# Ten input projection tiles of a two-block transformer kernel, unsplit and between the steps of its delta-rule stage

## The reference, cut to what matters

```python
proj = h @ w_in
qkv_a, z_a, b_a, a_a, qkv_b = split(proj)       # 1536, 512, 4, 4, 1536 columns
qkv_a = silu(causal_dwconv(qkv_a, conv_qkv_w))  # 4 heads of 128: gated delta rule
qa = l2norm(qa) * 128 ** -0.5;  ka = l2norm(ka)
g = -exp(a_log) * softplus(a_a + dt_bias);  beta = sigmoid(b_a)
o_a = rmsnorm(gated_delta_rule(qa, ka, va, g, beta)) * silu(z)
o_b = dilated_attention(qb, kb, vb)             # 8 heads of 64, from qkv_b
x = x + concat([o_a, o_b]) @ w_out
```

## Time and profile before

| | |
|---|---|
| three runs | 2054.92, 2056.27, 2057.14 us; median 2056.27 |
| the profiled execution | 2054.92 us, span 2053.1 us |
| busy over the span | TensorE 96%, its weight loads 77%, VectorE 62%, ScalarE 39% |
| instructions | 35683 |
| DMA | 164.68 MB, mean 80 GB/s |

### The profile page before, as it was taken

The page is one execution under the profiler, slowest core; times in us unless marked ns, Lnnn a source line. Parts: engine busy times, 40 slices in busy tenths (PEclk is TensorE's granted clock), DMA queues, the critical chain, the costliest instruction groups (busy, mean ns, idle before and its releaser), DMA issues.

```text
span 2053.1 us, 35683 instructions
## 1 busy us (share of the span) xinstructions
PE 1970.2 (96%) x15123; PEld 1587.1 (77%) x15123; DVE 1276.1 (62%) x2192; ACT 810.2 (39%) x1268; POOL 0.2 (0%) x4
## 2 busy tenths in 40 slices
PE   7998888899999999999999999999999999999998
PEld 6876555568888886788888888888887685888886
DVE  7622677557557565677777777777777734344444
ACT  5364333543334344534433443433434424332323
POOL 0000000000000000000000000000000000000000
PEclk9999899999999999999999999999999999999998
DMA  6331322233333322221211112121122441223221
GB/s 180 93 89 35 104 84 89 88 104 105 100 93 92 103 83 74 83 63 53 62 54 53 53 52 63 53 63 53 53 62 73 155 129 56 72 83 93 82 82 52
DMA packets 286160, 164.68 MB, mean 80 GB/s; under 512 B 6348, under 2 KB 283570, under 8 KB 286002
## 3 DMA queue, kind: packets, MB, share of 16 engines
q1 hardware_dynamic: 285492, 162.22, 26.8%
q10 hardware_dynamic: 510, 0.18, 0.0%
HBM read 160.29 MB, written 2.10 MB: 79 GB/s over the span
## 4 chain that ended last, share of the span: by engine, by line
PE 90%; DVE 5%; ACT 3%; issue 1%; DMA 0%; ACTq 0%; SPq 0%; DVEq 0%
PE bank L485 21%; PE bank L487 20%; PE bank L486 20%; PE bank L502 2%; PE bank L503 2%; PE bank L504 2%; PE bank L927 2%; PE bank L1092 1%; PE bank L975 1%; PE bank L958 1%; PE bank L468 1%; PE bank L549 1%; PE bank L547 1%; PE bank L548 1%; PE bank L935 1%
## 5 line engine op out<-in xcount | busy, mean ns | idle before, releaser
L485 PE MATMUL bank<-hh,wh 128*128 128x512 f32 x1384 | 562.1, 406 | 0.0
L1162 ACT ACTIVATE wh<-stage 128x1024 fp32r<-128x1024 f32 (+1 forms) x246 | 257.2, 1048 | 747.7 <-PE bank L487 489.2
L1686 DVE TENSOR_TENSOR wl<-stage,wh 128x1024 fp32r<-128x1024 f32 (+1 forms) x246 | 298.4, 1215 | 402.9 <-ACT wh L1162 402.9
L487 PE MATMUL bank<-hh,wl 128*128 128x512 f32 x1384 | 541.1, 391 | 0.0
L486 PE MATMUL bank<-hl,wh 128*128 128x512 f32 x1384 | 540.5, 391 | 0.0
L487 PEld LDWEIGHTS bank<-hh,wl 128*128 128x128 f32 x1384 | 260.1, 188 | 56.5
L485 PEld LDWEIGHTS bank<-hh,wh 128*128 128x128 f32 x1384 | 260.4, 188 | 55.5 <-issue 3.9
L486 PEld LDWEIGHTS bank<-hl,wh 128*128 128x128 f32 x1384 | 260.9, 188 | 48.7 <-issue 1.0
L485 PE MATMUL bank<-gh,wh 128*128 128x512 f32 x324 | 126.7, 391 | 0.0
L487 PE MATMUL bank<-gh,wl 128*128 128x512 f32 x324 | 126.2, 389 | 0.0
L486 PE MATMUL bank<-gl,wh 128*128 128x512 f32 x324 | 126.1, 389 | 0.0
(11 more groups left out here) (392 smaller groups left out, 2828.7 us busy)
## 6 DMA issues: line engine op xcount, KB each, us to landing
stage<-in_hg_w_in SPq DMA_DIRECT2D x80, 512.0 KB, 3.6
stage<-in_ada_w SPq DMA_DIRECT2D x48, 512.0 KB, 4.1
stage<-in_w_up SPq DMA_DIRECT2D x44, 512.0 KB, 3.7
stage<-in_ft_w_in SPq DMA_DIRECT2D x32, 512.0 KB, 3.9
stage<-in_w_in SPq DMA_DIRECT2D x28, 512.0 KB, 3.8
stage<-in_w_down SPq DMA_DIRECT2D x16, 512.0 KB, 3.9
stage<-in_hg_w_out SPq DMA_DIRECT2D x16, 512.0 KB, 4.2
stage<-in_ft_w_out SPq DMA_DIRECT2D x16, 512.0 KB, 4.0
```

Of the source, the lines that this page charges most:

```text
L485: pe.matmul(bank[t % NLIN][:], wh[:, s, k, :], xh[:, k, :], start=a, stop=False)
L487: mm = pe.matmul(bank[t % NLIN][:], wl[:, s, k, :], xh[:, k, :], start=False, stop=b)
L1162: do(A.activation(wh[:, l % NSPLIT, 0:nk, :], stage[:, u["slot"], 0:nk, :], ACT.Copy), "hi_ready")
L1686: do(X.tensor_tensor(wl[:, l % NSPLIT, 0:nk, :], stage[:, u["slot"], 0:nk, :], wh[:, l % NSPLIT, 0:nk, :].bitcast(F32), ALU.subtract), f"s ...
```

## The change

Tiles 18 to 27 leave the projection loop; `T_IN` is 18. The loop keeps qkv_a, z, and queries and keys of head pair 0 (`FIRST_PAIR`). The ten others (`MIDS`: queries and keys of pairs 1 to 3, values of all pairs) become "mid" units, computed unsplit, eight blocks each (one per slice k), between the steps of the delta-rule stage, by a table `FILL` (blocks placed early and late in step n). Values are computed with the tokens on partitions at once, so their transposes go. All mids accumulate in bank 2, ScalarE copies each finished tile (`mid_copy`). The raw units no longer sit in the odd steps but where `MOD_STEP` puts them, and the list of units, with it the order of loads and the slots, is interleaved anew. VectorE makes the whole activations (`whole_h`, eight sums) in chunk 0. The column sums are now two groups of four, after tiles 9 and 12, and use four banks and parts of `bqkv`; squares are taken after tiles 6 and 10; the gate products come after tiles 5, 7 and 14. Some buffers of the stage move so that `hh` and `hw` stay intact.

In the diff the wait on `mid_ev` by `(3, 6, 9, 10)[hp]` is `weigh`'s; the two pairs of `fill_first` and `fill_last` stand in step 0 (and so in step 7) and, behind T, in steps 1 to 6.

```diff
+T_IN = 18
+FIRST_PAIR = (0, 4)
+MIDS = (1, 5, 8, 2, 6, 9, 3, 7, 10, 11)
+FILL = {0: (1, 1), 1: (1, 2), 2: (1, 2), 3: (1, 2), 4: (1, 2), 5: (1, 1), 6: (1, 2), 7: (1, 2), 8: (1, 1),
+        11: (1, 3), 12: (1, 3), 13: (1, 3), 14: (1, 3), 15: (1, 3), 16: (1, 3),
+        19: (1, 3), 20: (1, 3), 21: (1, 3), 22: (1, 3), 23: (1, 3), 24: (1, 3),
+        27: (1, 3), 28: (1, 3)}
+MID_END = {2: 0, 5: 1, 8: 2, 12: 3, 14: 4, 16: 5, 20: 6, 22: 7, 24: 8, 28: 9}
+MOD_STEP = {1: 0, 3: 1, 5: 2, 7: 3, 9: 4, 10: 5, 17: 6, 18: 7,
+            24: 8, 25: 9, 26: 10, 27: 11, 28: 12, 29: 13, 30: 14, 31: 15}
...
+    mids = [dict(w="w_in", rows=(0, 8), col=O_B + m * P, lin=False, mid=i) for i, m in enumerate(MIDS)]
+    done = 0
+    for n in range(32):
+        step = []
+        if n in MOD_STEP:
+            step.extend(raws[2 * MOD_STEP[n]:2 * MOD_STEP[n] + 2])
+        if n in FILL:
+            if done % 8 == 0:
+                step.insert(0 if n % 8 in (0, 7) else len(step), mids[done // 8])
+            done += sum(FILL[n])
+        units.extend(step)
...
-                if t in range(16, 24, 2):
-                    col_sum(t - 16)
-                    col_sum(t - 15)
+                if t in (9, 12):
+                    for i in range(4):
+                        col_sum(i + (4 if t == 12 else 0))
...
-            for a in range(TT):
...
-                for j in range(4):
-                    mm = pe.transpose(bank[1 + a % 2][:, j * P:(j + 1) * P], bqkv[:, 8 + j, a * P:(a + 1) * P], ident[:])
-                mm.then_inc(S("vb_T"), 1)
+            def fill(n):
+                for _ in range(n):
+                    i, k = fed[0] // KT, fed[0] % KT
+                    fed[0] += 1
+                    u = mid_units[i]
+                    slot = u["slot"]
+                    if k == 0:
+                        pe.wait_ge(S(f"stage_in{slot}"), 16 * (u["load"] + 1))
+                        if i:
+                            pe.wait_ge(S("mid_ev"), i)
+                        if i >= 3:
+                            pe.wait_ge(S("ob_lo"), i // 3)
+                    if i == 0:
+                        pe.wait_ge(S("h_whole"), k + 1)
+                    if MIDS[i] < 8:
+                        mm = pe.matmul(bank[2][:], stage[:, slot, k, :], whole(k), start=(k == 0), stop=(k == KT - 1))
+                    else:
+                        for a in range(TT):
+                            mm = pe.matmul(bank[2][:, a * P:(a + 1) * P], hw[:, k, a * P:(a + 1) * P], stage[:, slot, k, :],
+                                           start=(k == 0 and a == 0), stop=(k == KT - 1 and a == TT - 1))
+                    if k == KT - 1:
+                        mm.then_inc(S(f"stage_free{slot}"), 1)
...
+                pe.wait_ge(S("mid_ev"), (3, 6, 9, 10)[hp])
...
                 attention_tail(n)
+                fill_first(n)
                 pe.wait_ge(S("eex"), c + 1)
...
                 scores(n + 1)
                 modulation(n)
+                fill_last(n)
...
                     modulation(n)
+                    fill_first(n)
                     attention_tail(n)
...
                     scores(n + 1)
+                    fill_last(n)
...
+            def mid_copy(n):
+                if n in MID_END:
+                    i = MID_END[n]
+                    u = mid_units[i]
+                    act.wait_ge(S(f"stage_free{u['slot']}"), u["load"] + 1)
+                    do(A.activation(bqkv[:, MIDS[i], :], bank[2][:], ACT.Copy), "mid_ev")
...
+            def whole_h(k):
+                do(X.tensor_tensor(whole(k), hl[:, k, :].bitcast(F32), hh[:, k, :].bitcast(F32), ALU.add), "h_whole")
```

More of the change, by code:

```diff
@@ L122, in make_units @@
     late = raws[32:]
-    for t in range(28):
-        add("w_in", (0, 8), t * P if t < 16 else O_B + (t - 16) * P, "h")
-    units.extend(raws[:32])
+    for t in range(T_IN):
+        add("w_in", (0, 8), t * P if t < 16 else O_B + FIRST_PAIR[t - 16] * P, "h")
+    mids = [dict(w="w_in", rows=(0, 8), col=O_B + m * P, lin=False, mid=i) for i, m in enumerate(MIDS)]
[9 more added lines that the diff above has]
+        units.extend(step)
     for n in range(KT):
@@ L335, in build @@
         T_OUT, T_UP, T_HG, T_HO, T_FT = FIRST["w_out"], FIRST["w_up"], FIRST["hg_w_in"], FIRST["hg_w_out"], FIRST["ft_w_in"]
-        MOD_STEP = {1 + 2 * j: j for j in range(16)}
         LATE_STEP = {0: 16, 1: 17, 2: 18, 3: 19, 5: 20, 6: 21, 7: 22, 8: 23}
-        late_units = [u for u in units if not u["lin"] and u["raw"] >= 32]
-        raw_last = {u["raw"] // 2: u for u in units if not u["lin"]}
+        raw_units = [u for u in units if "raw" in u]
+        late_units = raw_units[32:]
+        mid_units = [u for u in units if "mid" in u]
+        raw_last = {u["raw"] // 2: u for u in units if "raw" in u}
         WHOLE = {t: i for i, t in enumerate((T_UP, T_HG))}
@@ L590, in col_sum @@
                 pe.wait_ge(S("l2_sq"), i + 1)
-                if i >= 2:
-                    pe.wait_ge(S("l2_ln"), i - 1)
-                pe.matmul(bank[4 + i % 2][:], ones[:], sq[:, i % 2, :], start=True, stop=True
+                if i >= 4:
+                    pe.wait_ge(S("l2_ln"), i - 3)
+                pe.matmul(bank[4 + i % 4][:], ones[:], l2buf(i), start=True, stop=True
                           ).then_inc(S("l2_sum"), 1)
@@ L714, in modulation @@
                 if step in MOD_STEP:
-                    for _ in range(2):
-                        unit(units[pos[0]])
-                        pos[0] += 1
+                    for i in range(2):
+                        unit(raw_units[2 * MOD_STEP[step] + i])
             def attention_tail(n):
@@ L823, in _ @@
             weigh(3)
+            assert fed[0] == KT * len(MIDS)
+            pos[0] += 32 + len(MIDS)
             assert units[pos[0]]["lin"]
@@ L1298, in _ @@
             do(A.activation(silp[:, :, 1], V[:, ROWS["c_ctx"][0]:ROWS["c_ctx"][0] + 8], ACT.Silu), "silc_ready")
-            def square_pair(i, last):
-                if i < last:
-                    for n in (i, i + 1):
-                        col_square(n, qkv[:, n, :])
-            for t in range(28):
+            for t in range(T_IN):
                 finish_tile(t)
@@ L1345, in _ @@
                     do(A.activation(egc, bank[3][:, 80:96], ACT.Exp), "gate_act")
-            for a in range(TT):
-                act.wait_ge(S("vb_T"), a + 1)
-                do(A.activation(bqkv[:, 8:12, a * P:(a + 1) * P], bank[1 + a % 2][:].rearrange("p (j c) -> p j c", c=P), ACT.Copy), "vb_ev")
             def weights(n):
@@ L1781, in _ @@
             do(X.memset(raw[:, :, 0:3], 0.0), "set_dve")
-            for t in range(12):
+            for t in range(T_IN):
                 weights_behind(t)
@@ L1875, in _ @@
                 front(8 * c)
+                if c == 0:
+                    whole_h(2)
+                    whole_h(3)
                 dve.wait_ge(S("eex"), c + 1)
@@ L1889, in _ @@
                 do(X.copy_predicated(G["xt"][:], view(gmask[:, 0, :], [[0, 4], [1, P]]), G["lt"][:]), "x1")
+                if c == 0:
+                    for k in range(4, KT):
+                        whole_h(k)
+                    dve.wait_ge(S("h_whole"), KT)
                 dve.wait_ge(S("vk"), c + 1)
```

150 lines of the change are left out of this document (79 added, 71 removed).

## The result

The changed kernel takes **2068.56 us** (median of four runs, 2067.31 to 2069.41) against 2056.7 for the kernel before (2054.92 to 2057.15): ratio 1.0052, 95% interval 1.0035 to 1.0068. It is slower by some 12 us. The forecast was 2051.0 with a range of 2041 to 2063, so sign and range were both missed. On a second chip the same two kernels gave 1.0028 (1.0016 to 1.0040): slower again, by less. The profiled execution took 2069.41 us, span 2067.6.

The account below looks back on a forecast made before the run. TensorE was taken to bound the projection, with neither TensorE nor VectorE full in the delta-rule stage. Projection -57.4 plus stage +53.2 gave -4.2 us, 2050.7 against the profiled 2054.9; median put at 2051, range 2041 to 2063.

Parts of the forecast that it names:

- the clock behind the four waits for loads: Delta-rule stage, steps 3, 9, 25, 29: the sum counted the waits' idle time only, no slower clock behind them.
- front: Input projection up to the first scores: 28 tiles become 18 and value transposes go, -57.4 us, bounds -60 to -53.
- length of the waits: TensorE's idle time for late modulation loads and step 3's next tile weights: 11.6 us in all.
- the rest of the stage: Delta-rule stage less its load waits: 230.9 us of the 242.5 forecast, blocks and VectorE's new sums included.
- behind the stage: Everything after the delta-rule stage keeps its slots and its order: 0 us.
- rival D: ScalarE's chain between tiles 9 and 14 is longer by up to six table loads, 7.7 us: 2058.4 us; chance 0.04.
- The places of the waits: Modulation loads held by a projection tile's slot are waited for in steps 3, 9, 25 and 29.
- landing of 3.9 us: Held-back modulation loads land 3.9 us after the last product of the tile holding their slot, signal included.
- the half loss of clock counted at steps 9, 17 and 25: Steps behind the heads of chunks 1 to 3: blocks shorten the idle hole, so half the old clock loss stays.
- rival B: Clock stays at 2.4 GHz where blocks are dense and falls at no load wait: 6.0 us less, 2044.7; chance 0.27.
- Rival C: Clock falls at the four slot waits and again at each head, dense work at 1.2 GHz: +10.8, 2061.5; chance 0.20.
- Rival E: Stage hides nothing, blocks fully added to the old 189.3 us: +23.7, 2078.6 us; chance 0.02.

Follow-up runs that it names:

- e5: Changed kernel with the ten tiles' loads placed anew and the modulation of steps 3 and 5 moved to steps 2 and 4: 2041.98 us, ratio 0.9911.
- e3: Changed kernel with useless TensorE products put ahead of the awaited loads in steps 3, 9, 25 and 29: 2056.95 us, ratio 0.9984.
- e7: Kernel before the change, with three useless 512-column products in each chunk head ahead of the turned first inverse: ratio 0.9990.
- e8: e5 with the last of the ten tiles at place 33 of the load queue, not 34: ratio 0.9959.
- e6: Changed kernel with blocks moved into TensorE's holes, mainly chunk heads, loads and three modulation steps placed to suit: 2032.55 us, ratio 0.9865.
- e11: e6 with the two last blocks of step 1 moved to the end of chunk 0's head: 2030.82 us, ratio 0.9874.
- e4: Changed kernel with loads reordered, modulation steps moved and seven of eight blocks of each moved tile left out: 2019.39 us, ratio 0.9794.

## Why the prediction was wrong, step by step

The step that failed is the clock behind the four waits for loads: the forecast put it at nothing, and it measured +17.3 us. The other terms came out at -0.1 (front), +2.0 (length of the waits), -0.8 (the rest of the stage) and +0.2 (behind the stage) beside the forecast.

**The front was right.** Forecast -57.4, measured -57.5. ScalarE's chain was in time. The wait at tile 14 was 1.08 us where 2.3 were forecast:

```profile
120.82 0.40 PE L698 MATMUL bank<-gs,cst 128*128 128x16 f32 x2 [1.08 <-DVE gs L1870]
```

So rival D is out. By the 1.38 us of drain at each table load that the Trainium skill states (ScalarE: Activation LUTs, "What ACT_TABLE_LOAD costs") the chain would, as an estimate, have ended 8.3 us later. The trace disagrees: the wait is 1.08 us.

**The places of the waits were right, their length nearly.** The four steps were 3, 9, 25 and 29, with the next tile's weights late in step 3, as worked out. The sum was 13.6 us for 11.6, +2.0. The mis-sized term is the landing of 3.9 us, and it shows in two of the five: 4.20 us at step 9 for 3.0, and 1.91 for the next tile's weights in step 3 for 0.85. The others measured 2.69, 2.65 and 2.15 for 3.0, 2.5 and 2.2. The forecast took a load as it lands alone or in a pair, but a held-back slot releases three or four loads at once, and then they share the engines: the median landing of the modulation weights is 5.3 us in the changed kernel and 4.1 in e5, where no slot holds a burst back.

**The stage without its waits was right, by two errors that cancel.** The sum has 242.5 - 11.6 = 230.9 us without the waits; e5 has 230.1, though with two modulation steps moved. The blocks were dearer: groups of three ran at 2.77 us from the first to the next T, so 0.92 each, with single ones at 0.95 to 0.97, where 0.854 was taken from the inside of a dense tile. That is some 4 us over 80.

```profile
234.44 2.84 PE L720 MATMUL bank<-hw,stage 128*128 128x512 f32 x6
237.21 0.46 PE L829 MATMUL bank<-g_xx,g_lt 128*32 128x32 f32 x32
```

Against it, the half loss of clock counted at steps 9, 17 and 25 is absent where no wait comes: e5's steps 9, 17 and 25 take 5.4, 5.4 and 6.0 us. That is rival B's point, and it holds for a kernel that wasn't the one measured.

**The clock behind the waits was the miss.** The profiled stage is 18.5 us above the sum: +2.0 for the waits, -0.8 for the rest, +17.3 for slower products (18.4 by the busy sums; some 1 us of those lay where TensorE would have idled). By chunks against e5, with the waits taken off: 66.1 - 59.0 - 4.6 = 2.5; 62.7 - 55.8 - 4.2 = 2.7; 58.7 - 57.1 = 1.6; 73.5 - 58.2 - 4.8 = 10.5. Rival C had this mechanism and the sign, with 2.5, 1.4, 2.1 and 4.8. It got a chance of 0.20 and a price too low in chunk 3, where it assumed a fall of a few microseconds, and the fall outlasted steps 30 and 31. The argument in the record was in the wrong place. It let the clock fall behind the heads by precedent, and the earlier trace rows, and for the slot waits, as long and as idle, it counted the idle time only. Its one case against a fall was an idle 2.16 us in dense work; at 2.15 us idle the clock did fall here. Had the falls behind the waits been counted, C would have been the main line: 2061.5, still 8 us short of the profiled 2069.4. The forecast also named the heads as the place of all falls before; three others stood there, with no wait over 0.93 us ahead of them.

The rule of the Trainium skill beside it, that the clock follows how busy TensorE has lately been (TensorE: Matmul & The Clock Gate, "What's actually happening"), agrees in direction with e3 and e7, where useless work brought the clock up: 0.90 to 0.97 and 0.87 to 0.94 in the stage. No run here shows what decides how long a fall lasts.

**Rival E** (nothing is hidden) is out: 80 blocks raised the stage by 230.1 - 189.3 = 40.8 us in e5, eight `whole_h` among it, and not by 69.5; part of that is the higher clock, 0.98 for 0.87.

**What moves the sign.** The plan had +12 us as it stood, -14 with ten loads placed otherwise, and -27 with the blocks in the holes. The forecast of -4.2 was between them, since it saw the waits and not their echo.

## What to carry to other kernels

A wait of over 2 us in dense TensorE work must be priced twice, once as idle time and once as the half clock behind it; here one wait of 2.3 us cost 8.7 in one profiled execution, and about 10 in the medians of the ratios, with a smaller wait beside it. When work with long-held slots is interleaved with work with short-held ones in one in-order load queue, write out for each load which slot it waits for and when that comes free: one place in the list was worth 0.5% of the kernel. Put added work into the idle stretches first, where it is free and keeps the clock, and take its price from groups of the size that it will have, not from the inside of a dense tile.

## What the runs showed of the hardware

- Products that compute nothing can make a kernel faster: 14 of them in e3, some 12 us of TensorE time, and the stage was 12 to 14 us shorter.
- A fall isn't fixed by the wait ahead of it: 3.57 us idle was followed by some 3.3 us of lower clock, 2.15 and 2.29 us by about 14. The same head with 1.80 us idle has a fall in one kernel's profiled execution and none in another's. Three falls of the kernel before have no wait over 0.93 us ahead of them.
- The falls differ from execution to execution, it seems. e8 spread over 10.9 us in ten runs, where e5, e6 and e11 had 3.7, 2.6 and 3.6 in four each. But waits for loads alone don't decide it: e7 has none and spread over 13.0 us in ten, e4 has 0.7 us of them and spread over 14.4 in four. The granted clock of the whole execution goes with the time: in e7 0.987 at 2050.51 us and 0.979 at 2063.52, in e8 0.987 at 2044.56 and 0.982 at 2055.41.
